# An encoder trunk on one core: the heads' weights split a stage early, first latents and first keys loaded a stage early, memory tiles behind their token tiles

## The reference

```python
h = rmsnorm(x, ln_g[i])
p = h @ w_in_a[j]
q_lat, kv_lat, k_pe, q_mem, gate = jnp.split(p, [...], axis=-1)   # 384, 256, 32, 256, 1024 wide
# mla_mixer: 12 heads, 64 plain + 32 rotated columns, values 64 wide
q = rmsnorm((rmsnorm(q_lat, qlat_g) @ w_uq).reshape(B, S, 12, 96), q_norm_g)
q = concat([q[..., :64], apply_rope(q[..., 64:], cos, sin)])
kv = (rmsnorm(kv_lat, kvlat_g) @ w_ukv).reshape(B, S, 12, 128)
k_nope, v = kv[..., :64], kv[..., 64:]
k = rmsnorm(concat([k_nope, broadcast(k_pe)]), k_norm_g)
k = concat([k[..., :64], apply_rope(k[..., 64:], cos, sin)])
o = block_attention(q, k, v, 96 ** -0.5)          # softmax over all keys of the group
```

## Time and profile before

| | |
|---|---|
| median of the runs | 3456.26 us |
| the profiled execution | 3457.05 us |
| its span | 3455.3 us |
| TensorE busy | 3244.4 us, 94% |
| VectorE busy | 2024.7 us, 59% |
| ScalarE busy | 1707.5 us, 49% |
| GpSimd busy | 1398.5 us, 40% |
| 16 DMA engines, mean rate | 132 GB/s |

### The profile page before, as it was taken

The page is one execution under the profiler, slowest core; times in us unless marked ns, Lnnn a source line. Parts: engine busy times, 40 slices in busy tenths (PEclk is TensorE's granted clock), DMA queues, the critical chain, the costliest instruction groups (busy, mean ns, idle before and its releaser), DMA issues. The chain is left out here.

```text
span 3455.3 us, 46901 instructions
## 1 busy us (share of the span) xinstructions
PE 3244.4 (94%) x17548; PEld 2752.9 (80%) x17548; DVE 2024.7 (59%) x2857; ACT 1707.5 (49%) x2472; POOL 1398.5 (40%) x910
## 2 busy tenths in 40 slices
PE   7979979999999999999979997998999979999899
PEld 6978856777777777777769997786788869999787
DVE  4548878888888888888753333444333234333432
ACT  4436645777777777777744544102222225444200
POOL 1228856888888888888910000000110000000000
PEclk9989979999999999999989998998999989999999
DMA  7858983333213333321053233885323233322565
GB/s 285 307 211 311 328 281 73 63 68 64 50 41 63 68 65 68 64 59 36 11 200 110 89 111 89 243 229 185 140 97 108 81 144 126 107 91 85 165 192 157
DMA packets 380229, 454.75 MB, mean 132 GB/s; under 512 B 51704, under 2 KB 317304, under 8 KB 367728
## 3 DMA queue, kind: packets, MB, share of 16 engines
q1 hardware_dynamic: 380016, 451.91, 42.5%
HBM read 262.07 MB, written 189.64 MB: 131 GB/s over the span
## 5 line engine op out<-in xcount | busy, mean ns | idle before, releaser
L1277 POOL TENSOR_TENSOR at_acc<-at_acc,at_ph 128x1024 f32<-128x1024 f32 x288 | 690.6, 2398 | 76.1 <-ACT at_ph L1203 55.7
L1203 ACT ACTIVATE at_ph<-at_sc 128x1024 fp32r<-128x1024 f32 x408 | 418.5, 1026 | 322.8 <-PE at_sc L1123 322.8
L1311 DVE TENSOR_TENSOR at_pl<-at_sc,at_ph 128x1024 fp32r<-128x1024 f32 x408 | 498.5, 1222 | 129.7 <-ACT at_sc L1204 129.3
L1297 DVE TENSOR_REDUCE at_mx<-at_mxp 128x1 f32<-128x512 f32 x816 | 522.1, 681 | 25.8 <-PE at_mxp L1134 23.8
L1204 ACT ACTIVATE at_sc<-at_sc 128x1024 f32<-128x1024 f32 x408 | 416.0, 1020 | 0.0
L171 PE MATMUL gm_gate<-gm_h,gm_g_hi 128*128 128x256 f32 x1280 | 367.7, 287 | 6.4 <-DVE gm_g_lo L160 6.4
L172 PE MATMUL gm_gate<-gm_h,gm_g_hi 128*128 128x256 f32 x1280 | 362.1, 283 | 0.0
L173 PE MATMUL gm_gate<-gm_h,gm_g_lo 128*128 128x256 f32 x1280 | 361.9, 283 | 0.0
L1119 PE MATMUL at_sc<-at_qt,at_kt 97*128 97x512 f32 x816 | 330.5, 405 | 3.9 <-DVE at_pl L1311 1.9
L1121 PE MATMUL at_sc<-at_qt,at_kt 96*128 96x512 f32 x816 | 325.0, 398 | 0.0
L1148 PE MATMUL at_o_hi<-at_ph,at_v 128*128 128x512 f32 x816 | 322.3, 395 | 2.1 <-DVE at_half L1316 2.1
(11 more groups left out here) (240 smaller groups left out, 7297.1 us busy)
## 6 DMA issues: line engine op xcount, KB each, us to landing
gm_h<-hT SPq DMA_DIRECT2D x48, 1024.0 KB, 7.2
hT<-lat_n_h SPq DMA_DIRECT2D x28, 1024.0 KB, 7.2
qT<-hd_stq SPq DMA_DIRECT2D x60, 384.0 KB, 5.4
kT<-hd_stk SPq DMA_DIRECT2D x60, 384.0 KB, 4.7
at_qt<-qT SPq DMA_DIRECT2D x120, 192.0 KB, 3.0
sgT<-gm_sg SPq DMA_DIRECT2D x80, 256.0 KB, 2.1
ou_o<-omix SPq DMA_DIRECT2D x40, 512.0 KB, 6.3
ou_sg<-sgT SPq DMA_DIRECT2D x40, 512.0 KB, 7.4
```

Source lines behind the costliest of these rows:

```text
L1203: act.activation(ph[:, g], sc[g % 2][:], ACT.Exp, scale=SCALE).then_inc(p_hi, 1)
L1277: pool.tensor_tensor(acc[:, c.slot, :], f32(ph[:, (g - 1) % 4]).rearrange("p b n -> p (b n)") if t == 1 else acc[:, c.slot, :], now, ALU.a ...
L1297: dve.tensor_reduce(mx[:, n:n + 1], mxp[n % 2][:], AX.X, ALU.max).then_inc(mx_in, 1)
L1311: dve.tensor_tensor(pl[:, g], sc[g % 2][:], f32(ph[:, g]), ALU.subtract).then_inc(p_lo, 1)
```

## The change

Four things are done.

1. **Start and order in the latents.** The first gain has a semaphore of its own and is loaded alone; the two gains for memory rows are loaded behind the first store, and a scaling of a memory tile waits for them. On ScalarE the high parts of token tile i + 1 come ahead of the squares of the tiles to follow, the memory tile's behind them. TensorE's half turns of a memory tile stand ahead of k = 3 and k = 6.
2. **The heads' weights and first latents a stage early.** The split tiles (`ha_uq`, `ha_ukv`), the latents' buffers (`ha_lat`) and their semaphores belong to a space that is open over both stages. The latents' stage splits the five weights, one each in steps 2 to 6, loads the fifth piece at step 5, the memory stage's first pieces (3 MB) at step 13, and the first two tiles of latents at step 16. The heads start with the tables' loads.
3. **The first keys and queries a stage early.** `ka_q` and head 0's half of the keys, `ka_k`, live in a space on the other side of SBUF that is open over heads and attention. In the heads' second to last step SP loads queries of part 0, keys of the 16 tiles of the first group, high and low, and queries of part 1; behind the last stores the keys of tiles 16 to 19. In the attention `const_in` counts six fills, since the row of ones is filled in two tiles.
4. **In the heads' step** VectorE makes the first low part of turned keys ahead of the values' low part.

The instruction counts are otherwise the same. Cut to its core, the diff is:

```diff
@@ class NormTranspose
+        self.gains_in = [s.sem(f"n_gains{n}") for n in range(2)]
-    def load_gains(self, sp):
-        for tile, rows in zip(self.g, self.gains):
-            sp.dma_start(tile[:], rows.broadcast_to([P, D])).then_inc(self.g_in, 16)
+    def load_gains(self, sp, others):
+        for n in range(1, len(self.g)) if others else (0,):
+            sp.dma_start(self.g[n][:], self.gains[n].broadcast_to([P, D])).then_inc(self.gains_in[others], 16)
@@ def scale(self, dve, n)
+        if self.order[n][2] > 0:
+            dve.wait_ge(self.gains_in[1], 16 * (len(self.gains) - 1))
@@ new
+class HeadsAhead:
+    STEPS = 5
+    def __init__(self, s, plan, following):
+        self.w = Weights(s, plan, following)
+        self.lat = s.sb("lat", [P, 2, 2, QL + KVL], F32R)
+        self.lat_in = [s.sem(f"lat{u}") for u in range(2)]
+    def load(self, sp, u, rows):
+        sp.dma_start(f32(self.lat[:, u]), rows).then_inc(self.lat_in[u], 16)
+class KeysAhead:
+    def load_q(self, sp, qT, head, part, quad):
+        for a in range(2):
+            sp.dma_start(f32(self.q[0:QK, quad, a]).rearrange("d (t n) -> d t n", n=P),
+                         qT[part * 4:(part + 1) * 4, head // 4, :, head % 4, a].rearrange("t d n -> d t n")
+                         ).then_inc(self.q_load[quad], 16)
+    def load_first(self, sp, kT, a, b):
+        for n, sem in ((0, self.kh_load[0]), (1, self.kl_load[0])):
+            sp.dma_start(f32(self.k0[0:QK, n, a * P:b * P]).rearrange("d (t n) -> d t n", n=P),
+                         kT[a:b, 0, 0:QK, n, 0].rearrange("t p n -> p t n")).then_inc(sem, 16)
@@ latents, SP
                 norm.load(sp, 0)
-                norm.load_gains(sp)
+                norm.load_gains(sp, 0)
                 norm.load(sp, 1)
                 ...
                 norm.store(sp, 0)
+                norm.load_gains(sp, 1)
                 w.load(sp)
                 def step(i):
+                    if i == 5:
+                        ahead.w.load_rest(sp)
+                    if i == 13:
+                        ahead.w.load_following(sp)
                     ...
+                    if i == 16:
+                        for u in range(2):
+                            sp.wait_ge(stored[u], 16)
+                            ahead.load(sp, u, latT[u])
@@ latents, TensorE
-                        if beside and k in (2, 5):
-                            norm.turn(pe, beside[0], k // 5)
+                        if beside and k in (3, 6):
+                            norm.turn(pe, beside[0], k // 6)
@@ latents, ScalarE
                 def step(i):
+                    turned = list(norm.between(i, i + 1))
+                    for n in turned[:1]:
+                        for half in range(2):
+                            norm.round_hi(act, n, half)
                     for n in norm.between(i + 1, i + 2):
                         norm.square(act, n)
-                    for n in norm.between(i, i + 1):
+                    for n in turned[1:]:
                         for half in range(2):
                             norm.round_hi(act, n, half)
                     ...
+                    if 2 <= i < 2 + ahead.STEPS:
+                        ahead.w.round_hi(act, i - 2, i - 1)
@@ latents, VectorE
+                    if 2 <= i < 2 + ahead.STEPS:
+                        ahead.w.take_lo(dve, i - 2, i - 1)
@@ heads, SP
-                load_lat(Tile(0, 0))
                 ...
-                load_lat(Tile(0, 1))
-                w.load(sp)
                 def step(j, u):
                     ...
+                    if t.known and t.n == TILES:
+                        sp.wait_ge(q_st[0], 16 * PT_TILES)
+                        keys.load_q(sp, qT, 0, 0, 0)
+                        sp.wait_ge(k_st[0], 16 * PT_TILES)
+                        keys.load_first(sp, kT, 0, PT_TILES)
+                        keys.load_q(sp, qT, 0, 1, 1)
                 ...
+                keys.load_first(sp, kT, PT_TILES, TILES)
@@ heads, VectorE (w.take_lo(dve) and ScalarE's w.round_hi(act) are gone from the start)
+                    if t2.within(TILES):
+                        low_k(t2, 0)
+                    if t1.within(TILES):
                         value_lo(t1)
                     if t2.within(TILES):
-                        for c in range(G):
-                            low_k(t2, c)
+                        low_k(t2, 1)
+                        low_k(t2, 2)
@@ attention, SP
-                load_q(c0)
-                load_k(0)
-                load_q(c0.ahead(1))
                 load_v(0)
@@ build
+        with ExitStack() as early, Space(nc, "ka", side="right") as s3:
+            s2 = early.enter_context(Space(nc, "ha"))
...
+            heads(nc, K, A, ahead, keys, latT, kpe_all, qT, kT, vS)
+            early.close()
+            attention(nc, K, keys, qT, kT, vS, omix, sums)
```

More of the change, by code:

```diff
@@ L1006, in keys_loaded @@
         def keys_loaded(c):
-            return 16 * sum(len(list(key_pieces(n))) for n in range(c.head % 2, c.head + 1, 2))
+            first = 16 if c.head % 2 == 0 and c.n > 0 else 0
+            return first + 16 * sum(len(list(key_pieces(n))) for n in range(c.head % 2, c.head + 1, 2))
         def stored(c):
@@ L1029, in load_q @@
                 def load_q(c):
[L1030 to L1034 removed]
+                    keys.load_q(sp, qT, c.head, c.part, c.quad)
                 def load_k(head):
```

98 lines of the change are left out of this document (45 added, 53 removed).

## The result

The changed kernel takes 3464.06 us in the median of 17 runs (3460.69 to 3468.07), the kernel before 3458.56 us on the same chips (17 runs). The ratio is 1.0018, with a 95% interval of 1.001 to 1.0025: some 6 us slower. The prediction said 3451.2, within 3440 to 3460, and gave slower 6 in 100. Of the 12.9 us between 3451.2 and 3464.06, 2.3 are the base, which the prediction had at 3456.26.

The account below looks back on a forecast made before the run. TensorE was taken as busy for 187 of 207 us in the latents and 219 of 230 in the heads, leaving only gaps. -10.25 - 3.55 + 0 + 8.25 + 0.5 = -5.05 us: 3451.2 from 3456.26, range 3440 to 3460.

Parts of the forecast that it names:

- Start, -2.75: Latents' start: first scaling 3.65 us earlier with two gain loads moved; 2.75 us counted as saved, bounds 0 and 3.65.
- The +0.6 for the later square: Latents, step 0: rounding ahead of the square makes the next scaling later, +0.6 us, bounds 0 and 1.1.
- Order of rounding, -4.2 and -6.4: Latents: 4.25 us wait and half clock go, less a new 1.8 us wait; seven memory turns wait 0.4, not 1.30.
- Weights split in the latents, +3.1: Latents: splits at the end of steps 3 and 5 delay awaited low halves by 1.35 and 1.75 us; other three hidden.
- The 3 MB "at nothing": Latents, step 13: the queue has room for the memory stage's early weights, so their load costs nothing.
- Rival D: Latents: the 3 MB at step 13 hold up a token tile's load, +9.5 us, 3460.7; chance 0.09.
- Into the heads, -3.55: Heads' start: tables land 4.55 us sooner, a table step 1.5 shorter, half clock under tile 1's keys costs 2.5.
- Low keys ahead, 0: Heads' tiles: GpSimd's 11.7 us loop sets the period without the moved instruction, so 0; bounds -5.5 and +2.
- rival C: Heads: TensorE's wait, not GpSimd's loop, sets the period; 5.8 us more saved, 3445.4; chance 0.12.
- Into the attention, +8.25: Heads to attention: keys in early -3.85, last stores behind 4,608 pieces +10.7, two key loads +0.9, space closing +0.5.
- The small rest: Attention and after: unchanged from 530 us on, but for +0.5 us where a second space closes at the attention's end.
- The prediction's own sign of being wrong: Wrong if last stores land at their old distance, the tile's period falls to 11.4, or TensorE's latents waits exceed 10 us.

Follow-up runs that it names:

- e3: Changed kernel with the memory rows' two gains (1 MB) loaded behind the second half of the latents' weights, not ahead: 3460.97 us, 1.0013 of before.
- e4: Kernel before with only the order of rounding on ScalarE and TensorE's later half turns of memory tiles: 3448.07 us, 0.9973 of before.
- g3: Changed kernel, gains and most early loads moved, ones filled by GpSimd, weights split in steps 2, 4, 6, 8, 10, 3 MB spread over steps 12-17: 3434.57 us, 0.9936.
- e1: Changed kernel with the memory stage's first 3 MB loaded at the heads' start behind the rope tables, not at step 13: 3457.83 us, 1.0001 of before.
- f4: Changed kernel with the memory stage's six 0.5 MB pieces issued one per step in steps 8 to 13 of the latents: 3456.43 us, 1.0001 of before.
- i1: Changed kernel with the 3 MB still in step 13, but behind that step's two token tile loads and its store: 3461.31 us, 1.0012 of before.
- f1: Kernel before with only the first low part of turned keys ahead of the values' low part on VectorE: 3454.30 us, 0.9991 of before.
- e2: Changed kernel with the six early query and key loads behind the last keys' stores, own semaphore for tiles 16 to 19: 3458.80 us, 1.0004 of before.

## Why the prediction was wrong

- **Start, -2.75.** Too large by 2.1: the second half of the weights is split 0.66 us earlier. I took the queue as saved while it ran low, but the 1 MB went from ahead of one fence to ahead of the next; with it behind, e3 has that split 3.3 us earlier than before. The +0.6 for the later square was about right: in e4, which changes nothing else at the start, the third tile is turned at 32.68 and not 31.85.
- **Order of rounding, -4.2 and -6.4.** Right in mechanism, short in size: e4 has 8.9 for the two where 10.6 were said. Seven turns wait 0.40 each, as forecast. The new wait at the first memory tile was 2.64 and not 1.8 (2.22 in e4), and the half clock that was to go with the 4.25 us came back in part behind it: the mean granted clock is 0.57 from 46.5 to 50.5 in the changed kernel and 0.57 from 47.5 to 51.5 in e4.
- **Weights split in the latents, +3.1.** Right: 1.66 and 2.06 in place of 0.40, so 2.9, at the two places named. In g3, with the splits in other steps, those turns wait 0.40. What this part alone saves in the heads, no run shows.
- **The 3 MB "at nothing".** This is the step that failed: some 6 us by e1 and f4, about half of the miss. The cover named was that TensorE asks for that tile a step later. But TensorE did not wait for that tile; it waited for the low half of the tile before, which stands behind the late tile's scaling on VectorE. Rival D had it, with a chance of 0.09: the condition (the load lands later than VectorE's place for its scaling), the sign and the queue's time (the two loads of x took 9.6 us to land); its 9.5 us on the kernel were more than the 3.4 to 7.9 that the latents' ends of e1, f4 and i1 lie under those of the five profiles with the 3 MB ahead. That its 3460.7 lies near the measured 3464.06 is in part luck, since it took every other term as right.
- **Into the heads, -3.55.** Low by 0.9: the first root came 6.9 us sooner, and from the third root to the fifth 2.4 were lost (14.4 against 12.0), where 2.5 were said for the half clock under tile 1's keys. e4 and f1, whose start of the heads is the old one, lose 1.6 there too, so the half clock as its cause is likely and not shown. The tables started 6.5 us into the stage, not 7.9.
- **Low keys ahead, 0.** Wrong: 2.5 us were gained, about half of rival C. With those 2.4 lost, the changed kernel's first root to last is still 0.13 less than before; f1 and e4 give 3.1. GpSimd's only idle time was VectorE's scaling, but that scaling can itself come sooner; that the moved part is what made it wait is argued from the period and not traced. The two stretches of the heads together were 3.5 us better than forecast, and that hid as much of the miss.
- **Into the attention, +8.25.** Right in mechanism, +9.9 in size. 4,608 pieces held up the stores 11.1 us (487.82 to 498.96), where 10.7 were forecast; short was the landing of the last stores: 6.3 us from the end of their issue to the next key load, and not 5.1. VectorE's fills were the last fence, as said.
- **The small rest**, +1.1 behind the memory stage's start and +1.45 in the attention, is inside the scatter of these stretches over profiles.

The prediction's own sign of being wrong came true: TensorE's waits in the latents' stage sum to over 10 us, 13.8 for the low halves alone and 22.3 with the three other rows.

## What to carry to other kernels

A load that is issued early is paid for by whatever is issued behind it, and the payer is found by reading the queue and then the program of each engine that works on the late tile, for what stands behind that work: here VectorE's scaling, with a low half of another tile behind it. Early loads ahead of a stage's last stores held the stage's end up by their issue, 11.1 us here, so nothing belongs there that isn't needed first; and these small pieces are to be counted, not their bytes. Edits that gain and edits that lose can hide each other; taking them apart gave a kernel 22 us faster, where the four together were 6 us slower.

## What the runs showed of the hardware

Pieces of 512 bytes went at some 390 a microsecond in both kernels, 3925 packets in 10 us and 4335 in 11, at 199 and 200 GB/s, where 50 to 100 us before moved 332 GB/s in larger ones. A fill of one row took a time by its length on VectorE, 4.33 us for 5,120 elements before and 2.19 for 2,560, so splitting it in two tiles cost only some 0.5 us, the space between them:

```profile
502.21 4.33 DVE L1318 MEMSET at_kt<- 1x5120 f32 x1 [6.97 <-issue]
```

SP stood 6.50 us over the issue of two small loads of queries, at 492.41 in the changed kernel, with the pieces of the loads ahead still in the queue; a stage whose end includes SP's program ended later by it even where no store waited for them (e2).
